# Expert up weights in two 4 MB transfers of four neighbouring rows to a partition

## What is computed

```python
h = modulate(rms_norm(x, g_ffn), sh_f, sc_f)          # 256 x 1024
# router: 32 experts, 4 for each token
def expert_block(xb, e):                              # the tokens that chose e
    u = xb @ w1[e] + b1[e]                            # w1[e]: 1024 x 2048
    glu = minimum(u[:, ::2], 7.0)
    lin = clip(u[:, 1::2], -7.0, 7.0)
    a = glu * sigmoid(1.702 * glu) * (lin + 1.0)
    return a @ w2[e] + b2[e]                          # w2[e]: 1024 x 1024
```

## Time and profile before

| | us |
|---|---|
| median of three runs | 1875.69 |
| the profiled execution | 1876.69 |
| its span in the profile | 1874.9 |
| first issue for expert 1 to the landing of the last expert weights | 370.0 to 1272.4 |
| PE busy in the span | 1796.9 (96%) |
| mean rate of the DMA over the span | 315 GB/s |

### The profile page before, as it was taken

The page is one execution under the profiler, slowest core; times in us unless marked ns, Lnnn a source line. Parts: engine busy times, 40 slices in busy tenths (PEclk is TensorE's granted clock), DMA queues, the critical chain, the costliest instruction groups (busy, mean ns, idle before and its releaser), DMA issues.

```text
span 1874.9 us, 24256 instructions
## 1 busy us (share of the span) xinstructions
PE 1796.9 (96%) x9768; PEld 1135.4 (61%) x9768; DVE 773.1 (41%) x1146; ACT 572.0 (31%) x913; POOL 16.5 (1%) x33
## 2 busy tenths in 40 slices
PE   6999999999999999989999999989999999999998
PEld 3799888743333333333333333327988888978886
DVE  3867655512112111121111111116676656676665
ACT  4444554411011110010100111105655545545552
POOL 0000001000000000000000000000000000000000
PEclk9999999999999999999999999999999999999999
DMA  9976755999999999999999999999356556336552
GB/s 356 326 257 234 240 191 197 350 423 428 431 431 431 431 431 431 429 431 429 430 431 430 432 430 430 431 429 331 129 178 201 180 201 202 124 104 206 197 170 100
DMA packets 155691, 592.40 MB, mean 316 GB/s; under 512 B 6735, under 2 KB 85775, under 8 KB 129120
## 3 DMA queue, kind: packets, MB, share of 16 engines
q1 hardware_dynamic: 152896, 582.75, 78.9%
q0 software_dynamic: 2512, 8.45, 1.5%
q10 hardware_dynamic: 208, 0.15, 0.0%
HBM read 590.26 MB, written 1.07 MB: 315 GB/s over the span
## 4 chain that ended last, share of the span: by engine, by line
PE 81%; DMA 12%; DVE 4%; ACT 2%; issue 1%; ACTq 0%; SPq 0%; DVEq 0%
PE psum L1837 19%; DMA expert_ring<-in_w_mlp_dram 10%; PE psum L1855 9%; PE psum L452 9%; PE psum L392 7%; PE psum L394 7%; PE psum L393 7%; PE psum L451 4%; PE psum L1819 3%; PE psum L436 2%; PE psum L438 2%; PE psum L437 2%; PE psum L1875 2%; DMA mixer_ring<-in_w_in_dram 1%; PE psum L1826 1%
## 5 line engine op out<-in xcount | busy, mean ns | idle before, releaser
L1837 PE MATMUL psum<-shared,expert_arena 128*64 128x512 f32 x1536 | 340.2, 595 | 8.8 <-DMA shared<-in_w_mlp_dram 8.8
L452 PE MATMUL psum<-layer_x_parts,layer_w_hi 128*128 128x512 f32 x704 | 240.5, 396 | 0.4 <-DVE layer_x_parts L2202 0.4
L1837 PEld LDWEIGHTS psum<-shared,expert_arena 128*64 128x64 f32 x1536 | 106.2, 137 | 221.0 <-issue 202.9
L1663 DVE TENSOR_SCALAR expert_arena<-psum 128x512 f32<-128x512 f32 x32 | 22.1, 692 | 527.8 <-PE psum L1837 527.8
L1558 ACT ACTIVATE expert_arena<-expert_arena 128x512 f32<-128x512 f32 x32 | 20.1, 630 | 501.3 <-DVE expert_arena L1663 501.3
L451 PE MATMUL psum<-layer_x_parts,layer_w_lo 128*128 128x256 f32 x616 | 171.8, 279 | 0.0
L353 DVE TENSOR_TENSOR mixer_w_lo<-mixer_ring,mixer_w_hi 128x1024 fp32r<-128x1024 f32 x96 | 116.3, 1223 | 87.7 <-ACT mixer_w_hi L348 87.3
L353 DVE TENSOR_TENSOR layer_w_lo<-slots_ahead,layer_w_hi 128x1024 fp32r<-128x1024 f32 x96 | 116.8, 1223 | 84.8 <-ACT layer_w_hi L348 84.7
L348 ACT CAST mixer_w_hi<-mixer_ring 128x1024 fp32r<-128x1024 f32 x96 | 99.9, 1048 | 146.0 <-PE psum L394 76.0
L452 PEld LDWEIGHTS psum<-layer_x_parts,layer_w_hi 128*128 128x128 f32 x704 | 125.8, 188 | 24.6 <-DVE layer_x_parts L2202 0.8
L392 PE MATMUL psum<-layer_w_hi,layer_x_parts 128*128 128x512 f32 (+1 forms) x368 | 134.2, 365 | 1.0 <-DVE layer_x_parts L2202 1.0
(11 more groups left out here) (330 smaller groups left out, 2641.3 us busy)
## 6 DMA issues: line engine op xcount, KB each, us to landing
shared<-in_w_mlp_dram SPq DMA_DIRECT2D x98, 2048.0 KB, 19.2
expert_ring<-in_w_mlp_dram SPq DMA_DIRECT2D x64, 2048.0 KB, 23.0
mixer_ring<-in_w_in_dram SPq DMA_DIRECT2D x38, 1024.0 KB, 6.0
slots_ahead<-in_w_mlp_dram SPq DMA_DIRECT2D x15, 2048.0 KB, 24.5
mixer_ring<-in_w_ada_dram SPq DMA_DIRECT2D x22, 1024.0 KB, 5.8
slots_ahead<-in_w_ffn_in_dram SPq DMA_DIRECT2D x22, 1024.0 KB, 5.0
memory_kv<-in_w_mlp_dram SPq DMA_DIRECT2D x15, 1024.0 KB, 24.5
kept<-in_w_mlp_dram SPq DMA_DIRECT2D x15, 1024.0 KB, 26.7
```

The source lines that it names most:

```text
L452: last = self.nc.tensor.matmul(out, hi, both[:, k].rearrange("p h s -> p (h s)"), start=k == 0, stop=k == KC - 1)
L1837: last = nc.tensor.matmul(U[CAP * h:CAP * h + CAP, N * n:N * n + N], xg[:, k, j, :], expert_slot(M, k // 2)[:, at:at + N], start=False, st ...
```

## The change

An up load is now half of an expert, `4 * P` rows with four neighbouring ones to a partition (32 KB), into two slots that are neighbours in one tile. The slots are laid out anew: up halves in `shared` slots 0, 1 and `expert_ring` slots 0, 1; down halves 0 and 1 in `shared` slot 2 and `expert_ring` slot 2. From expert 2 on, SP waits for the second quarter of the half to be used and then issues one 4 MB transfer; for expert 0's second half and the whole of expert 1 it still issues quarters (`up_load_half`). PE waits once for each half, also where it came in quarters. All column steps go from two to four. Expert 0's first down half takes the place of its third up quarter in the early loads. The next layer's first load into `shared` waits for the down product of expert 30 as well.

```diff
-            for k in range(AHEAD):
-                up_load(sp, M, A, 0, k)
+            up_load(sp, M, A, 0, 0)
...
-            pool.dma_start(w_router.rearrange("p (s j) e -> p s (j e)", j=2), ...
+            pool.dma_start(w_router.rearrange("p (s j) e -> p s (j e)", j=4), ...
...
+PAIRS_UP = UP // 2
+HOMES = (("shared", 0), ("shared", 1), ("expert_ring", 0), ("expert_ring", 1), ("shared", 2), ("expert_ring", 2))
...
+def up_load(sp, M, A, e, a):
+    ring, at = HOMES[2 * a]
+    src = A["w_mlp1"][0, bass.ds(e, 1), 4 * P * a:4 * P * (a + 1), :].rearrange("o (p k) n -> p (o k n)", k=4)
+    sp.dma_start(M[ring][:, WIDE_SLOT * at:WIDE_SLOT * (at + 2)], src).then_inc(M["up_here"][a], 16)
...
-            def up_load_freed(i, e, k, free_first):
-                if free_first:
-                    sp.wait_ge(up_used, (i - 1) * UP + k + 1)
-                up_load(sp, M, A, e, k)
+            def up_load_freed(i, e, a):
+                sp.wait_ge(up_used, (i - 1) * UP + 2 * a + 2)
+                up_load(sp, M, A, e, a)
...
             def first_slots_early():
+                down_load(0, 0, 0, False, False)
                 sp.wait_ge(mixed["full"], mixed["merged"])
...
-                for k in range(AHEAD, UP):
-                    up_load(sp, M, A, 0, k)
+                up_load_half(sp, M, A, 0, 2)
                 sp.wait_ge(mixed["full"], mixed["products"])
-                for k in range(DOWN):
-                    down_load(0, 0, k, False, False)
+                up_load_half(sp, M, A, 0, 3)
+                down_load(0, 0, 1, False, False)
...
-                        at = 2 * P * (2 * part + k // 2) + k % 2
-                        last = nc.tensor.matmul(..., hn[:, t, at:at + 2 * P - 1:2], ...
+                        at = 4 * P * part + k
+                        last = nc.tensor.matmul(..., hn[:, t, at:at + 4 * P - 3:4], ...
...
-                    if k % 2 == 0:
-                        pe.wait_ge(up_here[k // 2], (i + 1) * 16)
+                    if k % 4 == 0:
+                        pe.wait_ge(up_here[k // 4], up_landed(i, k // 4))
...
                 sp.wait_ge(summed["up_used"], E * UP)
+                sp.wait_ge(summed["down_used"], (E - 1) * DOWN)
```

More of the change, by code:

```diff
@@ L1154, in on_tensor, with quarter @@
                         pe.wait_ge(table_here, 32)
+                    def quarter(row, at, i):
+                        if g in (3, 4):
+                            return row[:, at:at + N].rearrange("p (c h j) -> p h c j", h=2, j=2)[:, i % 2]
+                        return row[:, at + D // 4 * (i % 2):at + D // 4 * (i % 2 + 1)]
                     for i in range(4):
                         out = b[32 * i:32 * i + 32, 0:D // 4]
-                        nc.tensor.matmul(out, ones[:, 0:32], ada_sums[:, D // 4 * i:D // 4 * (i + 1)], start=True, stop=False)
+                        nc.tensor.matmul(out, ones[:, 0:32], quarter(ada_sums, N * (i // 2), i), start=True, stop=False)
                     for i in range(4):
@@ L1161, in on_tensor @@
                         row = 2 * g + i // 2
-                        last = nc.tensor.matmul(out, ident[0:12, row:row + 1].to_broadcast([12, 32]), b12[:, D // 4 * (i % 2):D // 4 * (i % 2 + 1)], start=False, stop=True)
+                        last = nc.tensor.matmul(out, ident[0:12, row:row + 1].to_broadcast([12, 32]), quarter(b12, 0, i), start=False, stop=True)
                 elif name == "gcol":
                     pe.wait_ge(late_here, 48)
-                    for j in range(2):
-                        last = nc.tensor.transpose(b[:, 4 * j:4 * j + 4], g_ffn_rows[:, j::2], ident[0:4, 0:4])
+                    for j in range(4):
+                        last = nc.tensor.transpose(b[:, 2 * j:2 * j + 2], g_ffn_rows[:, j::4], ident[0:2, 0:2])
                 elif name == "fcol":
@@ L1483, in one_round @@
                 if later:
-                    for k in range(UP):
-                        sp.wait_ge(down_used, i0 * DOWN)
-                        up_load(sp, M, A, 0, k)
+                    sp.wait_ge(down_used, i0 * DOWN)
+                    for a in range(PAIRS_UP):
+                        up_load(sp, M, A, 0, a)
                     for odd in range(2):
@@ L1491, in one_round @@
                     first_slots_early()
-                for k in range(UP):
-                    up_load_freed(i0 + 1, 1, k, True)
+                if later:
+                    for a in range(PAIRS_UP):
+                        up_load_freed(i0 + 1, 1, a)
+                else:
+                    for k in range(UP):
+                        sp.wait_ge(up_used, k + 1)
+                        up_load_half(sp, M, A, 1, k)
                 with sp.Fori(1, PAIRS - 1) as q:
@@ L1496, in one_round @@
                         e = sp.snap(q * 2 + odd)
-                        for k in range(UP):
-                            up_load_freed(i0 + e, e, k, True)
+                        for a in range(PAIRS_UP):
+                            up_load_freed(i0 + e, e, a)
                         for k in range(DOWN):
@@ L1764, in on_tensor @@
                     for k in range(4):
-                        at = 2 * P * (2 * half + k // 2) + k % 2
-                        last = nc.tensor.transpose(b[:, P * k:P * k + P], x_sb[:, t, at:at + 2 * P - 1:2], ident)
+                        at = 4 * P * half + k
+                        last = nc.tensor.transpose(b[:, P * k:P * k + P], x_sb[:, t, at:at + 4 * P - 3:4], ident)
                     last.then_inc(full, 1)
@@ L1816, in gather, with up_landed @@
                     for t in range(T):
-                        at = 2 * P * (2 * part + k // 2) + k % 2
-                        last = nc.tensor.matmul(gathered_bank(part, first_of_all)[:, P * k:P * k + P], hn[:, t, at:at + 2 * P - 1:2], pick[:, t].rearrange("p j s -> p (j s)"), start=t == 0, stop=t == T - 1)
+                        at = 4 * P * part + k
+                        last = nc.tensor.matmul(gathered_bank(part, first_of_all)[:, P * k:P * k + P], hn[:, t, at:at + 4 * P - 3:4], pick[:, t].rearrange("p j s -> p (j s)"), start=t == 0, stop=t == T - 1)
                 last.then_inc(gathered, 1)
+            def up_landed(i, a):
+                if isinstance(i, int) and i == 0:
+                    return (1 + a) * 16
+                return (i + 2 + a) * 16
             def up(i, pairs, j, ahead=None):
@@ L2737, in program @@
             "shared": sb("shared", [P, 12800]),
-            "up_here": [ctx.enter_context(nc.semaphore(f"up_here{k}")) for k in range(UP)],
+            "up_here": [ctx.enter_context(nc.semaphore(f"up_here{k}")) for k in range(PAIRS_UP)],
             "b12": sb("b12", [12, N]),
```

19 lines of the change are left out of this document (10 added, 9 removed).

## The result

The kernel after takes 1920.0 us (median of six runs, 1917.57 to 1927.49), the kernel before 1875.61 in runs beside it: +44.4 us, a ratio of 1.0233 (95%: 1.0223 to 1.0243). The forecast was 1883.0, +7.3, with a range up to 1889.5. The direction was right, the size was not: four fifths of the loss came from a term that the prediction had put at nothing.

What follows compares the result with a forecast made beforehand. The prediction took the experts to be bound by the DMA's stream of weights, where a dry queue is lost time. Its terms, 3.5 + 4.1 + 1.2 + 1.2 - 2.7 = +7.3 us, gave 1883.0 us, range 1876.5 to 1889.5.

Steps and rivals of the forecast that it cites:

- Columns, constants: Column steps going from two to four in PE's weight loads, and modulation rows: no cost, bounds -0.5 and +1 us.
- start, up(2): Expert 2's first half is issued 3.5 us later, leaving the DMA queue dry: loss 3.5 us, bounds 2.5 to 4.
- branch, up(18): Behind the branch, expert 18's load is issued later and the queue is dry: loss 4.1 us, bounds 0 to 6.
- end, up(31): Expert 31's load, queued directly behind expert 30's, is issued too late: loss 1.2 us, bounds 0 to 2.5.
- last products: PE's work on the last experts ends later behind the coarser halves: 1.2 us more, bounds 0 to 3.5.
- packets: 18 fewer packets for each engine and expert over 29 experts: 2.7 us gained, bounds 0 to 5.3.
- early loads: Reordered loads behind the mixer's attention, before the experts: cost 0, bounds 0 and 1 us.
- Next layer, constants: Added wait before the next layer's loads: cost 0, up to 2 us; modulation rows keep the same number of matmuls.
- (1): Rival: the gap at the branch does not form, all else stands; +3.2 us, 1878.9 us; chance 0.17.
- (2): Rival: larger packets delay small loads such as the router's bias; +4 us on top, 1887.0 us; chance 0.14.
- (3): Rival: packets cost far more, losses being paid from 19 ns each; at 30 ns, 1870.0 us; chance 0.08.
- (4): Rival: rows are cut at 16 KB anyway, so only two small packets go; +9.4 us, 1885.1 us; chance 0.06.

Runs made afterwards that it cites:

- after_flat: The changed kernel, but ScalarE writes the hidden state so that the gather's weight loads have a step of one: 1885.95 us against 1876.69, ratio 1.0051.
- before_step4: The kernel before with only the gather's column step set to four, transfers unchanged, so the experts' output is not the reference's: 1914.66 us, ratio 1.0202.
- same_waits_16k: `after_flat` with its waits and slots, but each half sent as two 2 MB transfers of 16 KB rows, issued together: 1886.36 us against 1875.88, ratio 1.0053.
- load_probe: The kernel before plus 96 extra float32 128x128 matmuls behind the router, eight for each of twelve forms and steps; instruction times measured, no kernel time given.
- quarters_then_half: `after_flat` with each expert's first half in two quarters, each with its own wait, second half still 4 MB: 1883.09 us against 1875.88, ratio 1.0035.

## Why the prediction was wrong, step by step

*Columns, constants: the step that failed.* It costed the step of four at nothing (-0.5 to +1 us), from weight loads of 209 and 210 ns. Those are transposes. The gather is a float32 product, and the trace of before had no product with a step of four; the bound should have come from the dearest thing in sight, not from a row with the same shape. It measured +1.85 us for each gather of 16 matmuls, 3.7 us for two experts. The rest of the sum was there to be read: PE had 27.2 us of work for an expert against 29.25 of DMA, 2.05 to spare, and 1.85 took nearly all of it. The 27.2 were read ahead of the branch; behind it the trace of before has 28.0 (56.02 for two), 1.24 to spare, and there 1.85 is more than all of it. A term bounded at 1 us, "as gathers lie on the path at the start", was one that changes the bound: 38 of the 44 us. The other terms do make the kernel slower, by 9.3 us, so the direction doesn't rest on luck.

*The other steps*, read from `after_flat`, where this one is taken out (DMA time of 4 MB: 9.75):

| step | predicted | measured | how read |
|---|---|---|---|
| start, up(2) | +3.5 | +3.5 | lands 14.2 after the one before it, less 9.75, less 1.0 that the kernel before loses there |
| branch, up(18) | +4.1 | +3.7 | 865.3 to 878.7 is 13.4, less 9.75 |
| up(19) | none | +1.8 | 8 MB land in 21.3 (888.4 to 909.7), less 19.5 |
| end, up(31) | +1.2 | +1.1 | 1239.7 to 1250.6, less 9.75 |
| last products | +1.2 | +1.2 | 24.7 us from the last wait to the end of the stage, before 23.5 |
| packets | -2.7 | -3.5 | 58.25 for two experts, before 58.49, over 14.5 |
| early loads | 0 | 0 to +1.8 | stream starts at 371.87, before 370.02 |

The sum is 7.8 without the last row and 9.6 with it; the time says 9.3 (6.4 to 12.8 by the interval). The term that had been missing is the second loss behind the branch. It isn't a gap like the first: the rate stays at 397 GB/s or more, and the first half of up(19) lands 14.2 us after its issue, where those into an empty queue took 12.4 to 13.2. Why these 8 MB are slower no run shows. Of the 1.8 us at the start 0.35 is a wait for the router's bias, and 1.4 is there when the first expert load is issued, at 313.55, before 312.14. The changed kernel has the same mixer and issues it at 311.73, and two kernels with the mixer of before show L1166 0.5 and 1.2 later than the earlier trace rows, so this is no effect of the change. That the rest of the forecast came so near, +7.3 against +9.3, is in part luck: the missing 1.8 and the packets, taken 0.8 too low, pull opposite ways.

*Next layer, constants.* The columns of the gain are now turned with four small matmuls where two had done, 0.61 us for 0.40; the prediction had counted only the modulation rows. Beyond that nothing of either shows: from the end of the stage to the end of the span `after_flat`, which keeps both, takes 1884.2 - 1285.7 = 598.5 us, the kernel before 1874.9 - 1276.5 = 598.4.

*Rivals.* (1), no gap at the branch: refuted by `after_flat`, where it costs 3.7 us and up(18) lands 12.6 after its issue; in the changed kernel itself the hole is mostly PE's, since `before_step4` has it too, with fine waits (253 GB/s for 243). (2), larger packets delay small loads: the first half is right. The bias, issued at 313.3, landed so late that PE waited for it:
```profile
DMA to landing us min/median/max: 12.8/12.8/12.8
```
```profile
326.14 0.61 PE L1171 MATMUL psum<-common_consts,shared 2*128 2x2 f32 x4 [0.22 <-DMA kept<-in_b_router_dram]
```
9.3 us became 12.8. By the Trainium skill, "DMA: Bandwidth & Descriptors", section "Queues, rings and completion order", engines alternate between queues a packet at a time; these rows agree. With 16 KB rows and the same waits it is 9.1 again (`same_waits_16k`). But it cost 0.2 to 0.35 us and not 4, as it passed the point from which it decides by no more than that. (3), packets of over 19 ns: 0.24 us over 36 packets is 6.7 ns for each, so refuted. (4), rows cut at 16 KB: refuted by the packet count. What came true was on no list: the step as the bound.

## What to carry to other kernels

Before a layout edit is costed at nothing, price every access pattern that it changes at the instruction that reads it, with a row of the same operation, not of the same shape; here the weight loads of float32 products on PE cost nearly the same up to a step of two, a third more at three and 70% more from four on. If no such row exists, take the engine's slack for one round of the loop as the price from which the term decides, and take it in every form of the loop (here 2 us for an expert ahead of the branch, 1.24 behind it). And reorder data where it is written once (ScalarE here, 2 us longer in all and off the path), not in each of the 32 gathers that read it.

No kernel here beat the one before. The larger packets saved at most 3.5 us and the coarser waits cost up to 11.3 (3.5 + 3.7 + 1.8 + 1.1 + 1.2, the 1.8 being the loss of unknown cause); small transfers at the start, the branch and the end with large ones between weren't tried.

## What the runs showed of the hardware

- Weight loads of 128x128 float32 (`load_probe`), in products: 192, 196, 261, 330, 335 ns with steps of 1, 2, 3, 4, 8; matmuls with such a step on the moving side: 275, 405, 413 ns with 1, 4, 8. Weight loads in transposes: 140, 209, 209, 193 ns with 1, 2, 4, 8.
- ScalarE, two activations of 128x1024 float32 together: 2.19 us in order, 2.36 with a read step of two, 4.18 with a step of four.
- After a wait of PE for the DMA the same 32 matmuls take 8.78 us in place of 7.09, at a granted clock of 0.70 to 0.90 over 5 us in which they start (`same_waits_16k`, `quarters_then_half`); in `after_flat`, with as many waits, they never do. What tells the two apart stayed open.
